# Hybrid SSD / Hyena block: order of the output projection and the norm of y inside it

## The reference, cut to what matters

```python
def rmsnorm(t, g):
    t32 = t.astype(jnp.float32)
    y = t32 * lax.rsqrt(jnp.mean(t32 * t32, axis=-1, keepdims=True) + NORM_EPS)
    return (y * g.astype(jnp.float32)).astype(t.dtype)

    y = rmsnorm(y.reshape(b, L, SSD_WIDTH) * jax.nn.silu(z.astype(jnp.float32)), norm_g).astype(z.dtype)
    g = hyena_op(hy, hy_conv_w, hy_conv_b, hy_filt, hy_bias)
    return jnp.concatenate([y, g], axis=-1) @ w_out
...
    x = x + mod_l[2] * o_l      # in effect: gate times projection, added to the residual
```

## Time and profile before

| | |
|---|---|
| median of 3 runs | 2379.95 us |
| profiled execution | 2386.81 us, of which span 2385.0 us |
| TensorE busy | 92% of the span, mean granted clock 0.939 |
| VectorE / ScalarE / GpSimd busy | 38% / 19% / 36% |
| the `out0` stage | from 895.2 to 1082.9 us of the span |

### The profile page before, as it was taken

How to read it: one execution, slowest core, us unless ns; L and a number is a source line. 1 busy time by engine, 2 the same in 40 slices (tenths; PEclk the granted TensorE clock), 3 DMA queues, 4 the chain that set the end, 5 groups by cost and what they waited for, 6 DMA issues and landing times.

```text
span 2385.0 us, 30305 instructions
## 1 busy us (share of the span) xinstructions
PE 2192.0 (92%) x11978; PEld 1731.1 (73%) x11978; DVE 905.8 (38%) x1252; ACT 443.5 (19%) x825; POOL 856.4 (36%) x460
## 2 busy tenths in 40 slices
PE   7968999899998995998999999998787998999997
PEld 2437766788887774887888888887574676888886
DVE  3553354420334767333212122234216664322334
ACT  1213111001244553003000001000204632100110
POOL 0274354422223766324222232222421124444442
PEclk7779999899998997998999999998898998999998
DMA  8313432334211001111111222112110011223222
GB/s 303 140 53 131 146 116 84 106 106 144 86 45 54 2 1 44 53 62 45 62 59 53 74 65 67 51 56 70 63 45 18 1 43 64 97 77 109 97 78 72
DMA packets 50750, 181.52 MB, mean 76 GB/s; under 512 B 5815, under 2 KB 6071, under 8 KB 49688
## 3 DMA queue, kind: packets, MB, share of 16 engines
q1 hardware_dynamic: 48288, 163.60, 20.6%
q10 hardware_dynamic: 1848, 13.52, 1.5%
q0 software_dynamic: 512, 2.95, 0.4%
HBM read 177.95 MB, written 2.10 MB: 75 GB/s over the span
## 4 chain that ended last, share of the span: by engine, by line
PE 83%; DVE 6%; POOL 6%; DMA 2%; ACT 1%; issue 1%; ACTq 0%; DVEq 0%; SPq 0%
PE psum L487 20%; PE psum L492 20%; PE psum L488 20%; PE psum L1068 2%; PE psum L1056 2%; PE psum L1085 2%; PE psum L554 1%; POOL weights_lo L2046 1%; PE psum L708 1%; DMA weights<-in_wall 1%; PE psum L893 1%; PE psum L918 1%; PE psum L676 1%; DVE normed L1793 1%; PE psum L638 1%
## 5 line engine op out<-in xcount | busy, mean ns | idle before, releaser
L2046 POOL TENSOR_TENSOR weights_lo<-weights,weights_hi 128x1024 fp32r<-128x1024 f32 (+1 forms) x232 | 514.1, 2217 | 1046.0 <-DVE weights_hi L1620 1046.0
L1620 DVE CAST weights_hi<-weights 128x1024 fp32r<-128x1024 f32 (+1 forms) x232 | 167.0, 721 | 928.2 <-PE psum L492 766.5
L492 PE MATMUL psum<-normed_lo,weights_hi 128*128 128x512 f32 x1760 | 511.9, 354 | 0.0
L487 PE MATMUL psum<-normed_hi,weights_hi 128*128 128x512 f32 x1088 | 394.5, 363 | 8.8 <-POOL weights_lo L2046 8.8
L488 PE MATMUL psum<-normed_hi,weights_lo 128*128 128x512 f32 x1088 | 376.8, 361 | 0.0
L492 PEld LDWEIGHTS psum<-normed_lo,weights_hi 128*128 128x128 f32 x1760 | 287.7, 191 | 16.9
L487 PEld LDWEIGHTS psum<-normed_hi,weights_hi 128*128 128x128 f32 x1088 | 206.6, 190 | 57.7 <-POOL weights_lo L2046 6.4
L487 PE MATMUL psum<-normed_first_hi,weights_hi 128*128 128x512 f32 (+1 forms) x672 | 235.6, 351 | 11.8 <-POOL weights_lo L2046 11.3
L488 PEld LDWEIGHTS psum<-normed_hi,weights_lo 128*128 128x128 f32 x1088 | 207.7, 191 | 35.3 <-issue 1.0
L488 PE MATMUL psum<-normed_first_hi,weights_lo 128*128 128x512 f32 (+1 forms) x672 | 215.8, 342 | 0.0
L487 PE MATMUL psum<-hidden_hi,weights_hi 128*128 128x512 f32 (+1 forms) x528 | 189.3, 358 | 0.0
(11 more groups left out here) (291 smaller groups left out, 3144.8 us busy)
## 6 DMA issues: line engine op xcount, KB each, us to landing
weights<-in_wall SPq DMA_DIRECT2D x264, 512.0 KB, 3.9
weights<-in_wall SPq DMA_DIRECT2D x32, 384.0 KB, 3.2
weights<-in_wall SPq DMA_DIRECT2D x32, 320.0 KB, 3.0
residual<-in_xT ACTq DMA_DIRECT2D x2, 3072.0 KB, 10.6
phase<-in_tab ACTq DMA_DIRECT2D x3, 1280.0 KB, 5.7
out_T<-normed SPq DMA_DIRECT2D x2, 1024.0 KB, 4.3
normed<-in_window ACTq DMA_DIRECT2D x1, 1536.0 KB, 16.4
normed<-in_window POOLq DMA_DIRECT2D x1, 1536.0 KB, 7.7
```

The source lines that it names most:

```text
L487: mm(acc[:, lo:hi], WH[:, b, k, :], high[:, lo:hi], start=st, stop=False)
L492: ins = mm(acc[:, lo:hi], WH[:, b, k, :], low[:, lo:hi], start=False, stop=en)
L1620: dve.tensor_copy(WH[:, b, 0:n, :], W[:, s, HALF * b:HALF * b + n, :]).then_inc(w_hi, 1)
L2046: TT(WL[:, s, at, :], W[:, s, at, :], WH[:, b, 0:width(gs[0], b), :].bitcast(f32), ALU.subtract).then_inc(w_lo, 1)
```

## The change

The first three blocks' convolution halves come first: two share job `G0` and run together tile by tile (`both_by_tile`, L503, which exists and is used elsewhere), the third is half 0 of job `G0+1`. Then come the three gated halves, then five jobs as before. The norm of y takes the short form: ScalarE squares into PSUM, VectorE adds the squares up into `temps` and TensorE does the token sums after tile 5 and the spread after tile 7 of block 0. The scalings read the norm from PSUM (`NP`). GpSimd waits for all products y*z before it begins with the low parts of g, and it makes the low weights of the next job between the low parts of y.

```diff
-    stage("out0", [("out0", 0, n) for n in range(8)])
+    stage("out0", [("halves", 0, ((0, 1), (1, 1))), ("halves", 0, ((2, 1), (0, 0))), ("halves", 0, ((1, 0), (2, 0)))])
+    stage("out0b", [("out0", 0, n) for n in range(3, 8)])
...
+        if kind == "halves":
+            out.append([(block, used[block]) for block, hyena in what if hyena])
+            for block, hyena in what:
+                used[block] += hyena
...
TensorE
-            half_ready([G0], 0, 0)
-            first = pair(pair_ready([G0], 0, 0))
-            tiles([G0], first, 0, KT, mixed, SEGS, True, False, mixed_waits)
-
-            norm_sums()
-            half_ready([G0], 0, 1)
-            tiles([G0], first, 1, KT, lambda k: mixed(KT + k), SEGS, False, True,
-                  [lambda k, wait=wait: wait(KT + k) for wait in mixed_waits])
+            def between_tiles(k, blocks):
+                if k == 5 and blocks == (0, 1):
+                    pe.wait_ge(yz_sums, 1)
+                    token_sums(6).then_inc(yz_summed, 1)
+                if k == 7 and blocks == (0,):
+                    pe.wait_ge(yz_rec, 1)
+                    token_spread(6).then_inc(yz_spread, 1)
+            both_by_tile([G0], 0, mixed, SEGS, mixed_waits, between_tiles, False)
+
+            gated = lambda k: mixed(KT + k)
+            gated_waits = [lambda k, wait=wait: wait(KT + k) for wait in mixed_waits]
+            half_ready([G0 + 1], 0, 0)
+            pe.wait_ge(yz_added, KT)
+            tiles([G0 + 1], pair(pair_ready([G0 + 1], 0, 0)), 0, KT, mixed, SEGS, True, False)
+            for g, b, u in ((G0 + 1, 1, 0), (G0 + 2, 0, 1), (G0 + 2, 1, 2)):
+                half_ready([g], 0, b)
+                tiles([g], pair(u), b, KT, gated, SEGS, False, True, gated_waits if u == 0 else None)
+
+            job_turns(pe, "out0b", 5, lambda gs, i, r: one_block(gs, i, mixed))
...
ScalarE
+            sqrt_table()
             for k in range(KT):
                 act.wait_ge(yz_ready, k + 1)
                 if k >= 2:
-                    act.wait_ge(sq_mm, k - 1)
-                run(T[:, k % 2, :], XBC[:, k, :], ACT.Square).then_inc(sq_ready, 1)
-            act.wait_ge(sq_mm, KT)
-            run(T[:, 2, :], NP, ACT.Sqrt, scale=1.0 / D, bias=vec("eps", 0)).then_inc(n_sqrt, 1)
+                    act.wait_ge(yz_added, k - 1)
+                run(TP if k % 2 else NP, XBC[:, k, :], ACT.Square).then_inc(yz_square, 1)
+            act.wait_ge(yz_summed, 1)
+            root()
...
VectorE
+            for k in range(KT):
+                dve.wait_ge(yz_square, k + 1)
+                square = TP if k % 2 else NP
+                if k:
+                    dve.wait_ge(yz_added, k)
+                    ins = TT(T[:, 3, :], T[:, 3, :], square, ALU.add)
+                else:
+                    ins = dve.tensor_copy(T[:, 3, :], square)
+                ins.then_inc(yz_added, 1)
+            dve.wait_ge(yz_added, KT)
+            dve.memset(MARK[:, 0:1], 0.0).then_inc(yz_sums, 1)
             dve.wait_ge(n_sqrt, 2)
-            ch.link(dve.reciprocal(T[:, 3, :], T[:, 2, :]))
+            dve.reciprocal(RS[1][:, 0:12], RS[0][:, 0:12]).then_inc(yz_rec, 1)
+            dve.wait_ge(yz_spread, 1)
             for k in range(KT):
-                STT(XBC[:, k, :], XBC[:, k, :], vec("sng", k), T[:, 3, :], ALU.mult, ALU.mult).then_inc(n_mul, 1)
+                STT(XBC[:, k, :], XBC[:, k, :], vec("sng", k), NP, ALU.mult, ALU.mult).then_inc(n_mul, 1)
+                if k in (2, 4):
+                    next_high([G0], 0, k // 2 - 1)
...
+                if name == "out0":
+                    next_high([G0 + 1], 0, 0)
+                    next_high([G0 + 1], 0, 1)
+                    for k in range(3):
+                        residual(X[:, k, :], k, k)
+                        read([G0 if k < 2 else G0 + 1], 0, k if k < 2 else 0, dve)
+                        ch.link(add_squares(X[:, k, :], lo, hi))
+                        if k < 2:
+                            next_high([G0 + 2], 0, k)
...
GpSimd
+            pool.wait_ge(yz_ready, KT)
             for n in range(2 * KT):
...
                 TT(YGL[j][:, k, :], src, YGH[:, j, k, :].bitcast(f32), ALU.subtract).then_inc(mix_lo, 1)
-            next_low("out0", 8, 2)
+                if n in (KT + 2, KT + 4):
+                    low([G0 + 1], 0, (n // 2 - 5,))
+            for g in (G0 + 1, G0 + 2):
+                low([g + 1], 0)
+            next_low("out0b", 5)
```

More of the change, by code:

```diff
@@ L81, in plan @@
     used, turn, out, last = [0, 0, 1], 0, [], None
-    for kind, layer, _ in JOBS:
+    for kind, layer, what in JOBS:
+        if kind == "halves":
+            out.append([(block, used[block]) for block, hyena in what if hyena])
+            for block, hyena in what:
+                used[block] += hyena
+            last = kind
+            continue
         n = job_blocks(kind)
@@ L334, in build_kernel @@
             kg_mm kg_free kg_sd kg_sq kg_ssq kg_root kd_mm kd_even kd_ev bias_in
-            sq_ready sq_mm norm_sqrt norm_mul hn_ready conv_first
+            yz_square yz_added yz_sums yz_summed yz_rec yz_spread norm_sqrt norm_mul hn_ready conv_first
             u_ready tp_mm tp_copied u_mm u_even u_sum u_prod p_half p_ready t5_in inv_mm g_ready
@@ L345, in build_kernel @@
          kg_mm, kg_free, kg_sd, kg_sq, kg_ssq, kg_root, kd_mm, kd_even, kd_ev, bias_in,
-         sq_ready, sq_mm, n_sqrt, n_mul, hn_ready, cv_act,
+         yz_square, yz_added, yz_sums, yz_summed, yz_rec, yz_spread, n_sqrt, n_mul, hn_ready, cv_act,
          u_ready, tp_mm, tp_copied, u_mm, u_even, u_sum, u_prod, p_half, p_ready, t5_in, inv_mm, g_ready,
@@ L575, in _ @@
             hn = lambda k: (HNH0[:, k, :], HNL[:, k, :])
[L577 to L583, removed]
             def norm_sum(n, segs=SEGS):
@@ L589, in norm_sum, with token_sums @@
                 pe.wait_ge(sums_ready, n + 1)
+                token_sums(tiles).then_inc(n_summed, 1)
+                pe.wait_ge(n_rec, n + 1)
+                token_spread(tiles).then_inc(n_spread, 1)
+            def token_sums(tiles):
                 for t in range(tiles):
@@ L592, in norm_sum, with token_spread @@
                              start=True, stop=True)
-                ins.then_inc(n_summed, 1)
-                pe.wait_ge(n_rec, n + 1)
+                return ins
+            def token_spread(tiles):
                 for t in range(tiles):
@@ L597, in norm_sum @@
                              C[:, IDENT, :], start=True, stop=True)
-                ins.then_inc(n_spread, 1)
+                return ins
             pe.wait_ge(silu_c, 1)
@@ L968, in _, with res_block @@
             mixed_waits = waits(mix_hi, 0, mix_lo, 0)
-            half_ready([G0], 0, 0)
-            first = pair(pair_ready([G0], 0, 0))
-            tiles([G0], first, 0, KT, mixed, SEGS, True, False, mixed_waits)
-            norm_sums()
-            half_ready([G0], 0, 1)
-            tiles([G0], first, 1, KT, lambda k: mixed(KT + k), SEGS, False, True,
-                  [lambda k, wait=wait: wait(KT + k) for wait in mixed_waits])
-            def res_block(name, rhs, segs=SEGS, by_tile=None, skip=0):
+            def between_tiles(k, blocks):
[15 more added lines that the diff above has]
+            job_turns(pe, "out0b", 5, lambda gs, i, r: one_block(gs, i, mixed))
+            def res_block(name, rhs, segs=SEGS, by_tile=None):
                 def body(gs, i, r):
-                    if isinstance(r, int) and r < skip:
-                        return
                     one_block(gs, i, rhs, segs, by_tile if len(gs) == 1 and isinstance(r, int) and r == 0 else None)
                 job_turns(pe, name, 8, body, peel=2 if by_tile else 0)
-            res_block("out0", mixed, by_tile=mixed_waits, skip=1)
             parts = lambda k: (HNH[:, k, :], HNL[:, k, :])
@@ L1861, in res, with residual @@
                     ch.link(dve.memset(T[:, 3, lo:hi], 0.0))
+                def residual(x, u, k):
+                    for j, (a, e) in enumerate(segs):
+                        ins = STT(x[:, a:e], pair(u)[:, a:e], column(layer, m, k, j), x[:, a:e],
+                                  ALU.mult, ALU.add)
+                    ins.then_inc(pair_free[u], 1)
+                if name == "out0":
[7 more added lines that the diff above has]
+                            next_high([G0 + 2], 0, k)
                 def body(gs, i, r):
@@ L1868, in body @@
                             next_high(gs, i, b if two else 1)
-                        k = r if not two else 2 * r + b
+                        k = r + 3 if name == "out0" else r if not two else 2 * r + b
                         if two:
@@ L1875, in body @@
                             dve.wait_ge(blocks_done, 2 * len(JOBS))
[L1876 to L1879, removed]
+                        residual(x, u, k)
                         if squares:
@@ L1886, in res @@
                 else:
-                    peel = 2 if name == "out0" else 0
```

(5 more changed lines are left out.)

## The result

| | before | changed |
|---|---|---|
| median | 2381.14 us (4 runs) | 2360.59 us (4 runs) |
| ratio | | 0.9916, 95% interval 0.9895 to 0.9937 |
| repeated, in a later group | 2381.01 us (9 runs) | 2359.31 us (5 runs), 0.9914, 0.9900 to 0.9927 |
| profiled span | 2385.0 us | 2355.5 us |

The kernel became faster by 0.8%, 15 to 25 us; forecast were 24.5 us (2355.5 us, range 2350.5 to 2366). The median before is that of four runs; the 2379.95 us given further up is that of the first three.

A forecast was written before the change was run, and what follows sets the result against it. TensorE bounds the kernel, so gains come from its waits and non-projection work before the run of fourteen halves. That run starts 24.9 us sooner, less 0.4 for the clock: 2379.95-24.5=2355.5 us, range 2350.5 to 2366.

The forecast's parts named there:

- Products: VectorE's eight products y*z, GpSimd waiting: two end at 902.9, six at 0.88 us each, done 908.2 (old clock).
- contention reading: VectorE and GpSimd hinder each other with two SBUF tensors on VectorE (subtractions 2.53 us), not with a PSUM input (1.89).
- Norm sums: VectorE's copy and additions of squares from PSUM: eight at about 1.0 us, done 916.3, signal 916.6 (old clock).
- dearer value: VectorE's norm additions at 2.57 us each if they met GpSimd, ending at 928.8 (old clock).
- First job: TensorE's two convolution halves together, tile by tile: clock rises at 914, tile 5 ends at 923.1 (old clock).
- Short norm: TensorE's six sums and six spreads at half the low-clock price: 1.4 and 1.5 us, spread done 928.1 (old clock).
- Third half: Third convolution half waits for GpSimd's weight split behind three subtractions: TensorE idles 8.0 us, until 938.2 (old clock).
- The rest: Fourteen halves after 938.2 (old clock) run without waits, as today's 119.8 us, plus 0.4 us for the low clock.
- Rival 2: First job stays at 1.2 GHz, GpSimd stays hindered: 12.9 us gained less 0.4, 2367.4 us; chance 0.24.
- Hindered additions: VectorE's norm additions meet GpSimd at 2.57 us each; alone they leave 18.8 us gained, 2361.2 us.
- Rival 3: The wait only moves: queued split after 958 (old clock) leaves under 5 us gained, 2375 to 2380 us; chance 0.04.
- Rival 4: Slower: in the fourteen halves casts come late behind VectorE's residuals and squares; at most 18.9 us slower, 2398.8; chance 0.04.

The follow-up runs named there:

- order_only: Changed kernel's new order of halves, but with the old norm (matrix-of-ones sums, full-tile root and reciprocal): stage 177.85 us, median 2373.6 us, ratio 0.9976 to before.
- no_product_wait: Changed kernel without GpSimd's wait for all products y*z: stage 170.7 us, median 2366.6 us, ratio 0.9948 to before.
- scale_from_sbuf: Changed kernel with the spread norm copied once to SBUF and read there by the scalings: stage 167.4 us, median 2360.8 us, ratio 0.9921 to before.
- early_split: Changed kernel with the third convolution half's weights cast and split before the low parts of y: stage 157.57 us, median 2355.7 us, ratio 0.9888 to before.
- first_tile_early: Changed kernel plus third half's weights split first, four tiles together, convolution tile 0's low part before first splits, sums after tile 4: 2346.2 us, 0.9857 of before.
- norm_only: Kernel before, old order of halves, with the short norm and GpSimd waiting for all products: stage 170.80 us, median 2365.0 us, ratio 0.9938 to before.

## Why the prediction was right

By its own steps, its times moved by 5.34 us to the changed trace (895.18 less 889.84):

- Products. Forecast end 902.9 (908.2 on the old clock), measured 903.2. The contention reading held in four kernels (changed, order_only, no_product_wait, scale_from_sbuf): two SBUF tensors meet GpSimd, a PSUM operand does not; scale_from_sbuf tests it directly. The row it came from was thinner than I read it: VectorE's instructions of the earlier trace rows end at 1102.96, so only 5.3 of GpSimd's 15.09 us lie beside them.
- Norm sums. Forecast 1.0 us each and a signal at 911.3; measured 1.05 us from start to start, signal at 911.56. The dearer value (2.57 us) was not needed.
- First job. Tile 5 forecast at 917.8, measured 919.16, 1.4 us late: the clock rose at 911.08, not at 908.7. That term was mis-sized; the next stage's start, from which I took it, has no wait inside, while here the clock rose at 900.83 and fell again at 904.25, before the wait ended.
- Short norm. The sums and the spread occupy TensorE for 1.26 and 1.25 us (919.16 to 920.42, 922.62 to 923.87); forecast 1.4 and 1.5, from half the low-clock price.
- Third half. The wait was forecast at 8.0 us, released by GpSimd's weights_lo; measured 8.53, released by it. The split took 2.80 us instead of 2.39, and VectorE's second cast, beside GpSimd, 2.22 instead of 0.69. The forecast's rule, two SBUF tensors, left the casts out: a cast reads one tensor, and it meets GpSimd too. Together the run began 1.9 us late (934.75 against 932.9).
- The rest. Fourteen halves forecast at 120.2, measured 119.51. So 24.5 less 1.9 plus 0.7: 23.3 us, and the stage shows 23.2. The misses are small, but some cancel: the late clock and the long split against cheaper sums and a quicker run.

The whole-kernel gain is about 20.5 us by the medians (interval 15.0 to 25.0, and 17.4 to 23.8 in the larger group), 4 less than forecast, and the stage's 23.2 lies within both. So 1.3 of the 4 us are in the stage; where the other 2.7 are stays open, lost outside the stage or never there, if the one profile before had a long stage: the rest of the program varies by more than that between single profiles (before the stage 888.6 to 895.2 us, after it 1296.3 to 1303.4, over ten profiles of kernels that have the same instructions there).

Rival 2 had both its halves tested. Hindered additions did not occur; the clock stayed low 2.4 us longer than forecast, not for the whole job. no_product_wait shows how near the case was: one wait of 8 us in front of the sums, and 6.3 us are gone. Rival 3's queue is real (early_split removes it and gains 6.9 to 7.2 us in the stage) but the split ended at 934.7 (940.1 on the old clock), far from the 958 that the rival needed. Rival 4: no wait of TensorE after 934.75 in the changed kernel.

## What to carry to other kernels

When a fast engine waits for a slow one, look at which neighbour hinders the slow one: reading one operand in PSUM instead of from a copy in SBUF was worth 3.0 us here (about 1 of it the copying), and letting the slow engine stand still until its neighbour was done 6.3 us, for one line each. Before moving a step on an in-order queue, list what stands in front of it; here the split of the next weights stood behind three subtractions although the engine had been idle 8 us before them. And compare stages, not spans, when the rest of the program varies by as much as the change is worth.

## What was not expected of the hardware

- GpSimd and VectorE both pay: a cast of 128x1024 in SBUF takes 0.69 us alone and 2.22 to 2.83 us beside GpSimd, and the split beside it 2.80 to 3.14 instead of 2.39 us (changed kernel and scale_from_sbuf).
- Moving 2.3 us of TensorE's matmuls to the front of a wait went with a clock that was different for far longer. With 2.9 us of matmuls and then a wait of 4.9 us (changed kernel) the clock was full from 900.83 to 904.25, all of it in the wait, and 1.2 GHz from there to 911.08. With 5.2 us of matmuls and then a wait of 2.6 us (first_tile_early) it was full from 900.66 to the end of the stage.
- Identical code before the stage took 888.6 to 895.2 us in ten profiles. The first 172 us ran at a granted clock of 0.74 to 0.83 from profile to profile, but the profile with 0.83 (norm_only) is not among the quickest. Why, no run here tells.
